# Positive part and square of the feed-forward rows in the halved chunks: from VectorE to ScalarE

## The chip, the cores and the metric

The kernel runs on one core of a Trainium2 chip. The metric is the device time of one execution in microseconds (us): the median of three runs of the kernel before is 2147.76 us (2145.67 to 2149.06). The engines are called as in the profile: PE is TensorE (matmuls; PEld are its weight loads), DVE is VectorE, ACT is ScalarE, POOL is GpSimd, SP is the engine that issues most of the loads.

## The reference

Two blocks of two layers each follow one another on 512 rows of width 1024, in float32: retention, latent attention, a chunk-gating mixer, dilated attention, each with its norms. In the second block each of the two layers ends with a feed-forward part, and this is what the change is about:

```python
y = _rms_norm(h, mlp_norm_g[layer])
h = h + jnp.square(jax.nn.relu(y @ w_up[layer])) @ w_down[layer]
```

The hidden width is 4096, so that the hidden rows are a 4096 x 512 matrix (features by positions), each element of which is cut at zero and squared between the two products.

## The kernel before, in words

Float32 accuracy is made of split operands: ACT rounds each operand to a high part (`hi`, a Copy to fp32r, line 1197), DVE (`lo`, line 1894) or, for weights, POOL (line 386) makes the low part as the difference, and PE adds three products (high with high, high with low, low with high). Weights come as 128x2048 panels: SP loads a panel into `RAW`, ACT writes `WH`, POOL writes `WL` in four parts of 128x512. There are two slots, used by turns.

The feed-forward part of a layer has 8 chunks of 512 hidden features. The first two are plain. The other six, the halved chunks, are made by a scheme with 7 products in place of 8 for each 256 features (`u` is 0 or 1). A halved chunk uses four panels: two up panels (u = 0, 1), then two down panels. Six halved chunks in each of two layers make 12. Of a chunk:

- PE runs `halved_panel` for u = 0 and u = 1, each with 7 products, then `down_panels`. The first down panel is taken by `tiles_together`: hidden tile k = 0 to 3 one after the other, 12 matmuls for each k, and before each k a wait until the low part of tile k (`HIDL`) is there. The second down panel follows without such waits.
- DVE runs `halved_up(i, 0)` and `halved_up(i, 1)`: it reads the products from the banks, adds them up into `T` (tile 0 and 1 for u = 0, tile 2 and 3 for u = 1; `near` is the first of the two and `far` the second), and cuts and squares each tile in place with one `scalar_tensor_tensor`, (max(t, 0)) * t, lines 2526 and 2532. Its signal `mlp_relu` counts these tiles. Between these steps it adds down results of the chunk before to `X` (line 2540), whose banks the u = 1 products want back, and in u = 1 it makes the low parts of tiles 0 and 1 (`low_hidden`), then those of tiles 2 and 3 at the end. After that it makes the sums of weight blocks for the next chunk (`sums_of_w`, lines 2478 to 2485).
- ACT takes its work in a written order: `WH` of the second up panel; `HIDH` of tile 0; `WH` of the first down panel; `HIDH` of tiles 1 and 2; `WH` of the second down panel; `HIDH` of tile 3; then the high parts of the weight sums (`EH`) with the next up panel between them.
- POOL makes `WL` of a panel in four parts as soon as ACT has its `WH`.

Behind the last halved chunk of the first of the two layers (L = 0) ACT also issues 16 DMAs of a bias table (`bias_table`, line 1693), then one more panel, and then the rows of the next norm (line 1265).

Of the kernel before, what the change touches and what calls it, by code (L numbers as in the profile page):

```python
# [146 lines left out]
def program(nc, panels, gains, xin, pin, pos, gn, decay, xtok, consts, every4, rel, onehot, wsT, bs, out, scratch, xsave):  # L147
    f32, f32r = mybir.dt.float32, mybir.dt.float32r
    ALU, ACT, AX = mybir.AluOpType, mybir.ActivationFunctionType, mybir.AxisListType
# [3 lines left out]
    with ctx:  # L153
        def sb(name, shape, dt=f32, c=ctx):
            return c.enter_context(nc.sbuf_tensor(name, shape, dt))

        S = Signals(lambda name: ctx.enter_context(nc.semaphore(name)))
# [34 lines left out]
        T = sb("T", [128, 4, 512])  # L192
# [1002 lines left out]
        def _(act):  # L1195
            def hi(dst, src):
                return nc.scalar.activation(dst, src, ACT.Copy)  # L1197
# [25 lines left out]
            def split_at(m):  # L1223
                split_panel(m, m % 2, m // 2)

            def split_in(i, per, m0):

                split_panel(i * per + m0, m0 % 2, i * (per // 2) + m0 // 2)
# [53 lines left out]
            def gained_tokens(L, rows):  # L1282
                for k in rows:
                    nc.scalar.activation(NORMED[:, k, :], X[:, k, :], ACT.Copy, scale=gain(f"mlp{L}", k))
                act.drain().then_inc(S["up_parts_hi"], 1)
# [401 lines left out]
            def mlp(L, n0):  # L1687
                def bias_table(kind):
                    rows = scratch[kind].rearrange("h q y -> h (q y)")
                    for b in range(128 // REPEATS):  # L1690
                        first = 127 - REPEATS * b
                        tile = rows[:, first:first + REPEATS * 255].rearrange("h (q y) -> q h y", y=255)[:, :, 0:128]
                        act.dma_start(TAB[REPEATS * b:REPEATS * b + REPEATS, :, KIND_AT[kind], :], tile)\
                           .then_inc(S["tab_loaded"], 16)

                def plain_chunk(c):
                    for f in range(4):
                        if f in (0, 3):
                            split_at(c * 4 + n0 + 2 + f // 3)
                        act.wait_ge(S["mlp_relu"], c * 4 + (4 * CHUNKS * L + f + 1))  # L1700
                        nc.scalar.activation(T[:, f, :], TG[:, f % 2, :], ACT.Square).then_inc(S["mlp_hid_f32"], 1)
                        act.drain()
                        hi(HIDH[:, f, :], T[:, f, :]).then_inc(S["mlp_hid_hi"], 1)
                        if c == 0 and f == 1:
                            gained_tokens(L, range(4, KD))

                def high_tokens():
                    act.wait_ge(S["up_parts_f32"], PARTS_SPLIT * L + 2)
                    hi(TOKH[:, :, :, :], TOK[:, :, :, :]).then_inc(S["up_parts_hi"], 1)

                def high_normed():
                    act.wait_ge(panel_used, n0 + 4 * PLAIN - 2)
                    hi(HH[:, 0:4, 0:256], NORMED[:, 0:4, 0:256])
                    hi(HH[:, 4:8, :], NORMED[:, 4:8, :]).then_inc(S["up_parts_hi"], 1)

                def high_sums(i, u):
                    act.wait_ge(S["up_parts_f32"], i * 2 + (PARTS_SPLIT * L + 3 + u))
                    hi(EH[:, u, :, :], SUMS[:, :, :]).then_inc(S["up_parts_hi"], 1)

                def high_of_chunk(i):  # L1720

                    high_sums(i, 0)
                    split_in(i, 4, n0 + 4 * PLAIN)
                    high_sums(i, 1)

                def halved_chunk(i):

                    def high_hidden(f):
                        act.wait_ge(S["mlp_relu"], i * 4 + (4 * CHUNKS * L + 4 * PLAIN + f + 1))
                        hi(HIDH[:, f, :], T[:, f, :]).then_inc(S["mlp_hid_hi"], 1)  # L1730

                    split_in(i, 4, n0 + 4 * PLAIN + 1)
                    high_hidden(0)
                    split_in(i, 4, n0 + 4 * PLAIN + 2)
                    high_hidden(1)
                    high_hidden(2)
                    split_in(i, 4, n0 + 4 * PLAIN + 3)
                    high_hidden(3)

                for c in range(PLAIN):  # L1740
                    plain_chunk(c)
                    if c == 0:
                        for j in range(2):
                            split_at(n0 + 4 + j)
                        high_tokens()
                high_normed()
                act.drain()
                high_of_chunk(0)
                with act.Fori(0, HALVES - 1) as i:
                    halved_chunk(i)  # L1750
                    high_of_chunk(i + 1)
                halved_chunk(HALVES - 1)
                if L == 0:
                    act.wait_ge(S["rows_stored"], 64)
                    for kind in range(4):
                        bias_table(kind)
                    split_at(n0 + 4 * CHUNKS)
# [132 lines left out]
        def _(ve):  # L1890
            v = nc.vector
# [527 lines left out]
            def mlp(L, n0):  # L2419
# [68 lines left out]
                def low_sums(i, u):  # L2488
                    ve.wait_ge(S["up_parts_hi"], i * 2 + (PARTS_HI * L + 5 + u))
                    lo(EL[:, u, :, :], SUMS[:, :, :], EH[:, u, :, :]).then_inc(S["up_parts_split"], 1)  # L2490

                def halved_up(i, u):
                    b0 = 4 - 4 * u
                    made, ahead = S["up_product"], 12 * HALVES * L + 6 * u
                    first, second, third = TG[:, u, 0:256], TG[:, u, 256:512], R[:, 256 * u:256 * u + 256]
                    near, far = T[:, 2 * u, :], T[:, 2 * u + 1, :]

                    def added(dst, b, to):

                        v.tensor_tensor(dst, B[b][:, 0:256], to, ALU.add)  # L2500
                        ve.drain()  # L2501
                        return v.tensor_tensor(dst, B[b][:, 256:512], dst, ALU.add)

                    ve.wait_ge(made, i * 12 + (ahead + 1))
                    v.reduce_sum(first, B[b0][:, :].rearrange("p (a n) -> p n a", a=2), AX.X)
                    ve.drain().then_inc(S["up_read"], 1)
                    if u == 0:
                        low_sums(i, 1)
                    ve.wait_ge(made, i * 12 + (ahead + 2))
                    added(second, b0 + 1, first).then_inc(free[b0 + 1], 1)  # L2510
                    ve.drain()
                    ve.wait_ge(made, i * 12 + (ahead + 3))
                    added(third, b0 + 3, second).then_inc(free[b0 + 3], 1)
                    ve.drain()
                    ve.wait_ge(made, i * 12 + (ahead + 4))
                    added(near[:, 256:512], b0 + 2, third).then_inc(S["up_read"], 1)
                    if u == 0:
                        down(i + (PLAIN - 1), 4, tiles=2)
                    else:
                        low_hidden(i * 4 + 4 * PLAIN, 0)  # L2520
                    ve.wait_ge(made, i * 12 + (ahead + 5))
                    v.reduce_sum(far[:, 0:256], B[b0][:, :].rearrange("p (a n) -> p n a", a=2), AX.X).then_inc(free[b0], 1)
                    ve.wait_ge(made, i * 12 + (ahead + 6))
                    added(near[:, 0:256], b0 + 1, third).then_inc(free[b0 + 1], 1)
                    ve.drain()
                    v.scalar_tensor_tensor(near, near, 0.0, near, ALU.max, ALU.mult).then_inc(S["mlp_relu"], 1)  # L2526
                    if u == 0:
                        down(i + (PLAIN - 1), 6, tiles=2)
                    ve.wait_ge(panel_used, i * 4 + (n0 + 4 * PLAIN + u + 1))
                    added(far[:, 256:512], b0 + 2, second).then_inc(free[b0 + 2], 1)  # L2530
                    ve.drain()
                    v.scalar_tensor_tensor(far, far, 0.0, far, ALU.max, ALU.mult).then_inc(S["mlp_relu"], 1)
                    if u == 1:
                        low_hidden(i * 4 + 4 * PLAIN, 1)

# [28 lines left out]
                with ve.Fori(0, HALVES - 1) as i:  # L2564
                    halved_up(i, 0)
                    halved_up(i, 1)
                    sums_of_w(i + 1, 0)
                    low_sums(i + 1, 0)
                    down(i + PLAIN, 0)
                    sums_of_w(i + 1, 1)  # L2570
# [413 lines left out]
```

## Time and profile before

| | |
|---|---|
| median of three runs | 2147.76 us (2145.67 to 2149.06) |
| the profiled execution's own time | 2148.23 us |
| its span | 2146.2 us |
| PE busy | 2116.5 us, 99% of the span |
| DVE busy | 1511.3 us, 70% |
| ACT busy | 914.6 us, 43% |
| POOL busy | 996.1 us, 46% |
| granted TensorE clock | full speed (2.4 GHz) over the whole span, 1.00 in the chunks looked at |

The chunks in question are at 1250 to 1491 us (first of the two layers) and 1891 to 2134 us (second). A row of the timeline gives start and duration in us, engine, line, operation, what it writes and reads, and, in brackets, how long the engine was idle before it and what ended that. Matmuls overlap, so a stalled PE shows little idle time in the busy columns: the distance of the same matmul from chunk to chunk is the better measure.

### The profile page before, as it was taken

Reading aid. Unit: us, or ns where it says so; the run is one execution under the profiler, and the core shown is the slowest. Engines: PE = TensorE matmul, PEld = TensorE weight load, DVE = VectorE, ACT = ScalarE, POOL = GpSimd, SP = SyncE. Lnnn points to the kernel's source line nnn. Section 1 sums busy time; section 2 is a strip of 40 time slices with the busy share of each in tenths; the row PEclk is TensorE's granted clock in tenths of the full one; section 3 lists DMA queues with packets and bytes.
Section 4 is the critical chain, followed back from the end, with each engine's and each line's share of the span. In section 5 each row is a group of like instructions: output and inputs, shape, how many; then the busy total and the mean of one; then the engine's idle time right before and its main releaser. Section 6 shows DMA issues by size and latency. Waiting matters only on the chain.

```text
span 2146.2 us, 30802 instructions
## 1 busy us (share of the span) xinstructions
PE 2116.5 (99%) x10510; PEld 1771.6 (83%) x10510; DVE 1511.3 (70%) x2143; ACT 914.6 (43%) x1315; POOL 996.1 (46%) x707
## 2 busy tenths in 40 slices
PE   9999999999999999999999999999999999999998
PEld 7888888778888888877888888888788888788886
DVE  7656556786777777778265788887565566788886
ACT  4433233555655555455445422224345445322233
POOL 4443544355434443425535655554443325555553
PEclk9999999999999999999999999999999999999999
DMA  6232222232222222232222222224212211222222
GB/s 227 87 103 83 95 74 91 89 126 101 87 78 78 78 78 81 87 117 97 100 79 98 98 98 98 98 98 137 98 66 73 79 60 59 98 98 99 97 99 77
DMA packets 38422, 202.16 MB, mean 94 GB/s; under 512 B 4395, under 2 KB 9643, under 8 KB 16076
## 3 DMA queue, kind: packets, MB, share of 16 engines
q1 hardware_dynamic: 29504, 191.46, 25.5%
q10 hardware_dynamic: 8844, 9.70, 1.5%
q8 instruction: 48, 0.79, 0.1%
q14 instruction: 26, 0.21, 0.0%
HBM read 195.90 MB, written 5.24 MB: 94 GB/s over the span
## 4 chain that ended last, share of the span: by engine, by line
PE 70%; DVE 15%; DVEq 7%; ACT 4%; issue 3%; POOL 1%; ACTq 1%; DMA 0%; POOLq 0%; SPq 0%
PE bank L468 12%; PE bank L474 11%; PE bank L469 11%; PE bank L455 8%; PE bank L456 8%; PE bank L457 8%; PE bank L947 2%; DVEq L2501 2%; DVEq L2482 1%; DVE X L2540 1%; PE bank L953 1%; DVE SUMS L2483 1%; ACT WH L1197 1%; ACT EH L1197 1%; DVE SUMS L1918 1%
## 5 line engine op out<-in xcount | busy, mean ns | idle before, releaser
L386 POOL TENSOR_TENSOR WL<-RAW,WH 128x512 fp32r<-128x512 f32 x700 | 989.8, 1446 | 1124.3 <-ACT WH L1197 1124.3
L1197 ACT ACTIVATE WH<-RAW 128x2048 fp32r<-128x2048 f32 (+1 forms) x190 | 336.4, 1773 | 239.1 <-PE bank L474 120.7
L468 PE MATMUL bank<-HB,WH 128*128 128x512 f32 x776 | 308.3, 397 | 0.8 <-DVEq L2595 0.8
L469 PE MATMUL bank<-HB,WH 128*128 128x512 f32 x776 | 302.8, 390 | 0.0
L474 PE MATMUL bank<-HB,WL 128*128 128x512 f32 x776 | 195.7, 395 | 0.0
L474 PEld LDWEIGHTS bank<-HB,WL 128*128 128x128 f32 x776 | 146.7, 189 | 32.7 <-issue 2.4
L468 PEld LDWEIGHTS bank<-HB,WH 128*128 128x128 f32 x776 | 146.0, 188 | 32.6 <-DVEq L2595 1.0
L469 PEld LDWEIGHTS bank<-HB,WH 128*128 128x128 f32 x776 | 145.9, 188 | 30.3 <-issue 1.0
L1197 ACT ACTIVATE HIDH<-T 128x512 fp32r<-128x512 f32 x64 | 40.2, 629 | 174.5 <-DVE T L2526 168.7
L1197 ACT ACTIVATE EH<-SUMS 128x1536 fp32r<-128x1536 f32 x24 | 35.7, 1489 | 175.3 <-DVEq L2486 175.3
L455 PE MATMUL bank<-HIDH,WH 128*128 128x512 f32 x256 | 100.5, 393 | 0.0
L457 PE MATMUL bank<-HIDH,WL 128*128 128x512 f32 x256 | 99.8, 390 | 0.0
L456 PE MATMUL bank<-HIDL,WH 128*128 128x512 f32 x256 | 99.7, 389 | 0.0
L468 PE MATMUL bank<-HIDH,WH 128*128 128x512 f32 x256 | 99.6, 389 | 0.0
L469 PE MATMUL bank<-HIDL,WH 128*128 128x512 f32 x256 | 99.6, 389 | 0.0
L2540 DVE TENSOR_TENSOR X<-X,bank 128x512 f32<-128x512 f32 x128 | 81.5, 680 | 8.6 <-PE bank L457 4.0
L1894 DVE TENSOR_TENSOR HIDL<-T,HIDH 128x512 fp32r<-128x512 f32 x64 | 68.2, 1081 | 24.9 <-ACT HIDH L1197 24.4
L947 PE MATMUL bank<-TOKB,EH 128*128 128x512 f32 x288 | 79.5, 397 | 0.9 <-DVE X L2540 0.5
L947 PE MATMUL bank<-HB,WH 128*128 128x512 f32 x288 | 78.4, 394 | 0.0
L455 PE MATMUL bank<-WH,HB 128*128 128x512 f32 x192 | 74.9, 390 | 0.7 <-ACT R L1197 0.7
L456 PE MATMUL bank<-WL,HB 128*128 128x512 f32 x192 | 74.7, 389 | 0.0
L457 PE MATMUL bank<-WH,HB 128*128 128x512 f32 x192 | 74.7, 389 | 0.0
(482 smaller groups left out, 5073.7 us busy)
## 6 DMA issues: line engine op xcount, KB each, us to landing
RAW<-panels SPq DMA_DIRECT2D x174, 1024.0 KB, 4.8
X<-xin SPq DMA_DIRECT2D x4, 512.0 KB, 8.0
xsave<-X ACTq DMA_DIRECT2D x4, 512.0 KB, 2.8
X<-xsave ACTq DMA_DIRECT2D x1, 2048.0 KB, 11.7
TAB<-scratch ACTq DMA_DIRECT2D x16, 128.0 KB, 3.3
out<-ACC SPq DMA_DIRECT2D x8, 256.0 KB, 2.3
RAW<-panels SPq DMA_DIRECT2D x2, 512.0 KB, 6.7
T<-xtok SPq DMA_DIRECT2D x2, 512.0 KB, 12.9
```

The lines of the kernel that those rows point to most:

```text
L386: gp.tensor_tensor(WL[:, s, cs], RAW[:, s, cs], WH[:, s, cs].bitcast(f32), ALU.subtract).then_inc(lo_ready, 1)
L455: nc.tensor.matmul(o, ah, bh, start=start, stop=False)
L456: nc.tensor.matmul(o, ah, bl, start=False, stop=False)
L457: return nc.tensor.matmul(o, al, bh, start=False, stop=stop)
L468: nc.tensor.matmul(o, wh[:, columns[k - k0]], xh[:, k, :], start=first and k == k0, stop=False)
L469: nc.tensor.matmul(o, wh[:, columns[k - k0]], xl[:, k, :], start=False, stop=False)
L474: end = nc.tensor.matmul(o, wl[:, columns[k - k0]], xh[:, k, :], start=False, stop=last and k == k1 - 1)
L947: nc.tensor.matmul(o[:, :].rearrange("p (a n) -> p a n", a=2), ah[:, cs], both(k), start=k == 0 and not onto, stop=k == 3, skip_group_chec ...
L1197: return nc.scalar.activation(dst, src, ACT.Copy)
L1894: return v.tensor_tensor(dst, src, high.bitcast(f32), ALU.subtract)
L2501: ve.drain()
L2540: end = v.tensor_tensor(X[:, f, :], X[:, f, :], B[b][:, :], ALU.add)
```

## The change

In `halved_up`, DVE no longer cuts and squares: a drain alone gives the signal `mlp_relu`, so this now says that the sums of the tile are in `T`. In `halved_chunk`, ACT does the work in two instructions in place, a Relu and a Square, each followed by a drain, ahead of the copy to `HIDH` that it made already. 48 `scalar_tensor_tensor` leave DVE (4 for each of 12 chunks), 96 activations come to ACT. The plain chunks, which already make the square on ACT, stay as they are.

```diff
                     def high_hidden(f):
                         act.wait_ge(S["mlp_relu"], i * 4 + (4 * CHUNKS * L + 4 * PLAIN + f + 1))
+                        nc.scalar.activation(T[:, f, :], T[:, f, :], ACT.Relu)
+                        act.drain()
+                        nc.scalar.activation(T[:, f, :], T[:, f, :], ACT.Square)
+                        act.drain()
                         hi(HIDH[:, f, :], T[:, f, :]).then_inc(S["mlp_hid_hi"], 1)
...
                     added(near[:, 0:256], b0 + 1, third).then_inc(free[b0 + 1], 1)
-                    ve.drain()
-                    v.scalar_tensor_tensor(near, near, 0.0, near, ALU.max, ALU.mult).then_inc(S["mlp_relu"], 1)
+                    ve.drain().then_inc(S["mlp_relu"], 1)
                     if u == 0:
                         down(i + (PLAIN - 1), 6, tiles=2)
                     ve.wait_ge(panel_used, i * 4 + (n0 + 4 * PLAIN + u + 1))
                     added(far[:, 256:512], b0 + 2, second).then_inc(free[b0 + 2], 1)
-                    ve.drain()
-                    v.scalar_tensor_tensor(far, far, 0.0, far, ALU.max, ALU.mult).then_inc(S["mlp_relu"], 1)
+                    ve.drain().then_inc(S["mlp_relu"], 1)
                     if u == 1:
                         low_hidden(i * 4 + 4 * PLAIN, 1)
```

On ACT, in the loop over halved chunks, from the second up panel to the copies of tiles 1 and 2, this is how the rows differ (+ is the changed kernel):

```order
 L1197 ACTIVATE WH<-RAW 128x2048
 L1729 REGISTER_ALU
+L1730 ACTIVATE T<-T 128x512
+L1732 ACTIVATE T<-T 128x512
 L1197 ACTIVATE HIDH<-T 128x512
 L1203 REGISTER_ALU
 L1197 ACTIVATE WH<-RAW 128x2048
 L1729 REGISTER_ALU
+L1730 ACTIVATE T<-T 128x512
+L1732 ACTIVATE T<-T 128x512
 L1197 ACTIVATE HIDH<-T 128x512
 L1729 REGISTER_ALU
```

The two new instructions stand ahead of each copy, and so ahead of the panel that follows it.

On DVE, at the end of u = 1, the rows before were these, from the sums of tile 2 to the first sum of weight blocks:

```order
L2502 TENSOR_TENSOR T<-bank,T 128x256
L2526 SCALAR_TENSOR_TENSOR T<-T 128x512
L2529 REGISTER_ALU
L2500 TENSOR_TENSOR T<-bank,TG 128x256
L2502 TENSOR_TENSOR T<-bank,T 128x256
L2532 SCALAR_TENSOR_TENSOR T<-T 128x512
L2439 REGISTER_ALU
L1894 TENSOR_TENSOR HIDL<-T,HIDH 128x512
L2439 REGISTER_ALU
L1894 TENSOR_TENSOR HIDL<-T,HIDH 128x512
L2477 ISA
L2478 TENSOR_TENSOR SUMS<-RAW 128x512
```

In the changed kernel (its lines stand 4 lower) the same place reads:

```order
L2506 TENSOR_TENSOR T<-bank,T 128x256
L2532 REGISTER_ALU
L2504 TENSOR_TENSOR T<-bank,TG 128x256
L2506 TENSOR_TENSOR T<-bank,T 128x256
L2443 REGISTER_ALU
L1898 TENSOR_TENSOR HIDL<-T,HIDH 128x512
L2443 REGISTER_ALU
L1898 TENSOR_TENSOR HIDL<-T,HIDH 128x512
L2481 ISA
L2482 TENSOR_TENSOR SUMS<-RAW 128x512
```

Nothing else has moved on DVE; the two low parts at the end now stand right behind the sums, and wait there for ACT.

## Rows read from the trace of the kernel before

**Rows 1.** The page's first part: busy us (share of span) xinstructions.

```profile
PE 2116.5 (99%) x10510; PEld 1771.6 (83%) x10510; DVE 1511.3 (70%) x2143; ACT 914.6 (43%) x1315; POOL 996.1 (46%) x707
```

**Rows 2.** Windows, first hidden matmul to the next chunk's: us, then PE, PEld, DVE, ACT, POOL.

```profile
1259.57:1301.07 41.50, 41.50 (x211) 35.17 (x209) 35.60 (x50) 12.62 (x10) 22.49 (x16) 1.00 0.29 101
1301.07:1343.05 41.98, 41.82 (x209) 35.33 (x209) 36.09 (x51) 12.61 (x10) 22.50 (x16) 1.00 0.29 100
...
1426.98:1468.76 41.78, 41.78 (x210) 35.34 (x209) 36.25 (x51) 12.61 (x10) 22.99 (x16) 1.00 0.29 100
sum 209.19, PE 208.74 PEld 176.51 DVE 180.08 ACT 63.08 POOL 112.91; mean PE 41.75 PEld 35.30 DVE 36.02 ACT 12.62 POOL 22.58
```

**Rows 3.** Timeline of PE, three places: start us, us, what, idle before.

```profile
1301.07 0.49 PE L455 MATMUL bank<-HIDH,WH 128*128 128x512 f32 x1
...
1309.35 0.39 PE L455 MATMUL bank<-HIDH,WH 128*128 128x512 f32 x1
...
1335.89 0.50 PE L947 MATMUL bank<-TOKB,EH 128*128 128x512 f32 x1 [0.16 <-DVE X L2540]
```

**Rows 4.** Timeline of DVE in the second halved chunk.

```profile
1291.96 0.69 DVE L2526 SCALAR_TENSOR_TENSOR T<-T 128x512 f32<-128x512 f32 x1
...
1299.28 2.26 DVE L1894 TENSOR_TENSOR HIDL<-T,HIDH 128x512 fp32r<-128x512 f32 x2
...
1302.55 0.42 DVE L2502 TENSOR_TENSOR T<-bank,T 128x256 f32<-128x256 f32 x1
...
1305.29 0.68 DVE L1894 TENSOR_TENSOR HIDL<-T,HIDH 128x512 fp32r<-128x512 f32 x1
1306.78 1.44 DVE L1894 TENSOR_TENSOR HIDL<-T,HIDH 128x512 fp32r<-128x512 f32 x1 [0.80 <-ACT HIDH L1197]
1308.39 1.52 DVE L2478 TENSOR_TENSOR SUMS<-RAW 128x512 f32<-128x512 f32 x1 [0.17 <-issue]
1309.84 1.77 DVE L2479 TENSOR_TENSOR SUMS<-RAW 128x512 f32<-128x512 f32 x1
...
1313.39 0.69 DVE L2485 TENSOR_TENSOR RAW<-RAW,SUMS 128x512 f32<-128x512 f32 x1
```

**Rows 5.** Timeline of ACT in the same chunk.

```profile
1293.23 1.90 ACT L1197 ACTIVATE WH<-RAW 128x2048 fp32r<-128x2048 f32 x1
...
1303.79 0.63 ACT L1197 ACTIVATE HIDH<-T 128x512 fp32r<-128x512 f32 x1 [7.66 <-DVE T L2526]
1304.33 1.90 ACT L1197 ACTIVATE WH<-RAW 128x2048 fp32r<-128x2048 f32 x1
1306.14 0.61 ACT L1197 ACTIVATE HIDH<-T 128x512 fp32r<-128x512 f32 x1
```

**Rows 6.** Timeline of POOL in the same chunk: the low parts of two panels.

```profile
1295.29 5.11 POOL L386 TENSOR_TENSOR WL<-RAW,WH 128x512 fp32r<-128x512 f32 x4 [3.83 <-ACT WH L1197]
...
1306.39 1.28 POOL L386 TENSOR_TENSOR WL<-RAW,WH 128x512 fp32r<-128x512 f32 x1 [6.00 <-ACT WH L1197]
```

**Rows 7.** Timeline of ACT in a plain chunk: Square, drain, copy.

```profile
1173.62 0.63 ACT L1701 ACTIVATE T<-TG 128x512 f32<-128x512 f32 x1
1174.34 0.63 ACT L1197 ACTIVATE HIDH<-T 128x512 fp32r<-128x512 f32 x1
```

**Rows 8.** Timeline of ACT behind the last halved chunk of L = 0.

```profile
1471.96 1.90 ACT L1197 ACTIVATE WH<-RAW 128x2048 fp32r<-128x2048 f32 x1
1473.05 0.85 ACTq L1693 DMA_DIRECT2D TAB<-scratch  x2
...
1481.04 1.92 ACT L1197 ACTIVATE WH<-RAW 128x2048 fp32r<-128x2048 f32 x1 [6.66 <-issue]
1482.86 0.70 ACT L1265 ACTIVATE HB<-X,G 128x512 fp32r<-128x512 f32 x1
```

**Rows 9.** Timelines of DVE and PE where that layer's next norm begins and ends.

```profile
1483.60 1.37 DVE L1907 SCALAR_TENSOR_TENSOR HB<-X,G,HB 128x512 fp32r<-128x512 f32 x1 [4.24 <-ACT HB L1265]
...
1503.33 1.13 PE L520 MATMUL bank<-SUMS,ONES 128*128 128x512 f32 x2 [0.62 <-DVEq L1920]
```

## The prediction

> **What bounds the kernel now.** The page's first part comes first: PE is busy for 99% of the span, DVE for 70%, ACT for 43% [rows 1]. That speaks for PE as the bound and for DVE and ACT work as free, and for most of the kernel it is so. It has to be checked in the halved chunks themselves, and busy shares don't do it, since overlapping matmuls hide a stall. So the second view is a table of windows, cut at the first matmul of each chunk that reads the hidden tiles [rows 2]. The first window lasts 41.50 us, the next three 41.98 (one row stands for them), the last 41.78. The work of PE is the same in all. So PE by itself needs about 41.4, and in steady state something else, slower by 0.5 us a chunk, sets the pace.
>
> The third view, PE's timeline, shows where: a product of u = 1 waits for a bank that DVE's L2540 gives back, and the first hidden matmul lasts 0.49 us in place of 0.39, as it is issued just when the low part of tile 0 has come [rows 3]. Fourth, the timelines of DVE, ACT and POOL in one chunk [rows 4 to 6]: DVE hardly waits for PE there; it goes round a ring of its own, with ACT and POOL in it: sums of a tile, square, ACT's copy, low part, weight sums, next chunk. This ring of 41.97 us is the bound, with PE half a microsecond behind. So the change is priced along the ring.
>
> **Price of a stage.** On ACT, Square, drain and copy follow each other by 0.72 us [rows 7]. A Relu has no row; I take it as another 128x512 activation with a drain, the same 0.72. Its bounds are 0.54 (the step from copy to the next panel without a drain, 1304.33 less 1303.79 [rows 5]) and 0.80 (the 0.70 of an activation with a scale for each partition [rows 8], and the 0.09 from end to start in rows 7). So the copy of a tile starts 1.44 us after the Relu does. On DVE a square takes 0.69 [rows 4]; I take back 0.15 to 0.2 for the signal, which now comes from a drain with a register step behind it (such gaps are 0.17 before L2478), so each removal frees about 0.5 us.
>
> **One chunk, step by step.** Let t = 0 be 1291.96, when DVE begins to square tile 0. The Relu begins there too, as the same drain releases it.
>
> First, before u = 1. ACT's copy of tile 0 starts at 1.44, and the panel behind it at 1.98 (it was 1293.23, so 1.27). POOL began 2.06 after that panel (1295.29) and takes four parts of 1.28, a little less back to back [rows 6]; now they end at about 5.3, 6.55, 7.8 and 9.05 if nothing comes between.
>
> Second, the low parts of tiles 0 and 1. DVE asked for the first at 1299.28, t = 7.32, in POOL's last part, and the two took 2.26. Two squares less bring this to about 6.26. That lies in POOL's second part. What happens then is read at the end of the chunk: the low part of tile 3, issued at 1306.78 during a POOL part that ended at 1307.67, lasted 1.44 instead of 0.68 and ended 0.55 after that part [rows 4, 6]. The next two DVE steps, 1.52 and 1.77, show the same again and again: the engines take turns, a DVE step ends 0.55 after the POOL part, and a POOL part 1.15 after the DVE step. So: low part 0 at 6.55 + 0.55 = 7.1, a POOL part to 8.25, low part 1 at 8.8. It was 1299.28 + 2.26, t = 9.58, so tile 2 is reached 0.77 earlier.
>
> The Trainium skill, page "SBUF — State Buffer", section "Who interferes with whom", says that a VectorE instruction with two SBUF inputs and a GpSimd instruction that reads SBUF exclude each other for a whole instruction, and that issue order decides who blocks. The trace agrees (1.44 against 0.68). By that rule POOL's third part, which waits first, goes in front of low part 1; the turn taken above rests on the rows.
>
> Third, tile 2. Its sums ended at 1302.97, t = 11.01; now 10.24. The Relu starts at 10.33, the copy at 11.77 (it was 11.83): two squares and a turn of POOL pay for the longer path. The second down panel starts at 12.31 (12.37).
>
> Fourth, tile 3: nothing pays here. Relu, Square and copy all stand behind that panel on ACT. The copy started 1.81 after the panel; now a Relu starts there, at 14.12, and the copy 1.41 later, ending at 16.16. Low part 3 then asks at 16.2, in POOL's second part (15.65 to 16.9), and ends at 17.46. Before, it ended at 1308.22, t = 16.26. So 1.2 us later.
>
> Fifth, the weight sums. They met three more POOL parts after low part 3, now two. Last sum: 17.46, POOL to 18.6, first sum 19.15, POOL 20.3, second 20.85, third 21.63, fourth 22.39. It was 22.12. The ring goes from 41.97 to 42.24, **0.27 us longer**, although DVE has 2.8 us less to do.
>
> **Sum.** Five passages between six chunks give 5 x 0.27 = 1.35 per layer. In the last chunk low part 3 is a further 1.2 later. Before, it ended 1.13 ahead of the matmul that waits for it (1309.35 [rows 3]), of which I leave 0.23 for signal and weight load, so 0.9 of cover. A layer's feed-forward part ends 1.35 + 1.2 - 0.9 = 1.65 later.
>
> For L = 0 another path is longer. ACT's 16 bias-table DMAs stood in front of a panel at 1481.04, and this in front of the next norm's rows, on which DVE waited 4.24 us and at whose end PE waits [rows 8, 9]. The first DMA went out 1.09 after the second down panel's start (1473.05), as soon as the copy of tile 3 was released. Now it also stands behind two drains: it goes out with that copy, 1.81 + 1.41 = 3.22 after the panel, 2.13 later. With 1.35 for the ring and 0.06 back, 3.4 us, which replaces 1.65.
>
> Together 3.4 + 1.65 = 5.05. The profiled execution took 2148.23 us (span 2146.2, the rest around it unchanged), 0.5 above the median; from the median 2147.76 this gives **2152.8 us**. Where bounds matter: a stage of 0.54 takes 0.5 off the copy of tile 3 and lets it meet the end of POOL's first part, so that the ring loses nothing (about +1); one of 0.80 puts 0.16 on tile 2 and on tile 3's copy, and the ring is some 0.2 to 0.3 longer still, +3 on the sum.
>
> **Rivals.**
> Fewer turns: low part 1 follows low part 0 without a POOL part between. Then it ends at 7.7, tile 2 is 1.1 us earlier still, the ring falls to 41.1 and PE's 41.4 becomes the bound. It gains 209.19 - 5 x 41.42 = 2.1 in each layer; the DMAs go out 1 us earlier than now. About 2144.7, faster than before. For it speaks that the two low parts followed each other at once in rows 4, against it that POOL had nothing left to do there, and that it had its turn between L2478 and L2479.
> A missed turn: if low part 0 asks 0.3 us later than reckoned, it misses the end of POOL's second part at 6.55 and waits for the third. Everything behind it comes 1.26 later, the ring is 43.5; 6 x 1.26 per layer, 15 more, 2168. The margin is 0.29 with a drain's gap uncertain by about 0.1 twice.
> Exchange at face value: each swap costs its own difference, 1.44 - 0.69, on tiles 2 and 3 of 12 chunks, 18 us, 2166. The Trainium skill, "ScalarE: Activation LUTs", section "Rules for kernel authors", gives relu, max and mul to VectorE and would point this way. Against it: the time that tile 2 gets back in the first to third steps.
> A cover that holds: ACT's stages are a bit shorter or DVE's relief a bit larger, so that ring and PE keep pace; only part of the DMAs' delay is left, 0 to +3, 2149.
>
> **How the numbers follow.** A measurement of this kernel tells 0.2%, 4.3 us, from no change. The forecast, +3 to +8, has a chance of 0.60, and 0.4 of this lies above 4.3 us. Fewer turns 0.14, of which 0.09 gains more than 4.3 us (the relief of L2540's banks adds to it); a missed turn 0.08; face value 0.04; a cover that holds 0.14. So slower 0.40 + 0.08 + 0.04, about 0.53; faster 0.09; within the bound 0.38. The range of the forecast alone is 2150.5 to 2156; 8 in 10 needs the cases beside it, 2145 to 2159.
>
> **What would show it.** The windows between first hidden matmuls are 42.2 us in steady state. The low part of tile 2 ends earlier against the first hidden matmul and that of tile 3 about 1 us later; PE now stalls before the first matmul of k = 3, and no more for L2540's bank. On DVE the low parts of tiles 0 and 1 have a POOL part between them. The first bias-table DMA goes out 3.2 us after the last panel's start instead of 1.09. Windows of 41.4 would show the ring gone and the forecast wrong; windows of 43.5 a missed turn; windows of 42.2 with an unchanged total would mean that the later path behind L = 0 has cover that I didn't see.

## The result and the profile after

The changed kernel takes 2153.95 us (median of seven runs, 2151.85 to 2155.46) against 2147.76 of the kernel before (seven runs, 2145.34 to 2149.06): a ratio of 1.003 with a 95% interval of 1.0021 to 1.0039, so between 4.5 and 8.4 us slower. The profiled execution took 2153.95 us with a span of 2151.9, 5.7 more than the span before. All lines of VectorE in this kernel stand 4 lower than before.

The page's first part, to be put beside [rows 1]:

```profile
PE 2116.9 (98%) x10510; PEld 1769.4 (82%) x10510; DVE 1474.6 (69%) x2095; ACT 974.1 (45%) x1411; POOL 1001.5 (47%) x707
```

DVE has 37 us less to do, ACT 60 more, PE the same. By busy time alone nothing is lost; in device time 6 us are. The windows from first hidden matmul to first hidden matmul, first of the two layers, answer to [rows 2]:

```profile
1258.94:1300.37 41.43, 41.43 (x211) 35.19 (x209) 32.02 (x46) 17.57 (x18) 22.12 (x17) 1.00 0.30 101
1300.37:1342.45 42.08, 41.71 (x210) 35.10 (x209) 32.68 (x47) 17.56 (x18) 22.80 (x17) 1.00 0.28 100
...
1384.63:1426.85 42.22, 41.73 (x211) 35.10 (x209) 32.81 (x47) 17.57 (x18) 22.92 (x17) 1.00 0.28 99
...
sum 210.08, PE 208.31 PEld 175.61 DVE 163.57 ACT 87.83 POOL 113.77; mean PE 41.66 PEld 35.12 DVE 32.71 ACT 17.57 POOL 22.75
```

The reader is to see that the windows have become longer (42.2 in place of 41.97) while of the engines' busy times in them only ACT's is clearly longer. PE, three places, beside [rows 3]:

```profile
1300.37 0.40 PE L455 MATMUL bank<-HIDH,WH 128*128 128x512 f32 x1
...
1309.11 0.49 PE L455 MATMUL bank<-HIDH,WH 128*128 128x512 f32 x1 [0.37 <-DVE HIDL L1898]
...
1335.44 1.09 PE L947 MATMUL bank<-TOKB,EH 128*128 128x512 f32 x4
```

The first hidden matmul no longer waits (0.40 in place of 0.49), nor does L947 for the bank of the down results; the matmul of k = 3 now does, for the low part of tile 3. It stands 8.74 us behind the first (1309.11 less 1300.37), where it would stand 8.21 behind without a stall (as in the experiment with tiles 0 and 1 below): 0.5 us in this chunk, 0.6 in the later ones. With the 0.1 that the stalled matmul itself lasts longer, this is nearly all that the windows have over PE's own 41.43. On DVE, ACT and POOL the second halved chunk reads as follows; the views are those of [rows 4 to 6].

```profile
1297.95 2.43 DVE L1898 TENSOR_TENSOR HIDL<-T,HIDH 128x512 fp32r<-128x512 f32 x2
...
1303.96 0.69 DVE L1898 TENSOR_TENSOR HIDL<-T,HIDH 128x512 fp32r<-128x512 f32 x1 [1.01 <-ACT HIDH L1197]
1307.68 1.30 DVE L1898 TENSOR_TENSOR HIDL<-T,HIDH 128x512 fp32r<-128x512 f32 x1 [3.03 <-ACT HIDH L1197]
...
1313.20 0.69 DVE L2489 TENSOR_TENSOR RAW<-RAW,SUMS 128x512 f32<-128x512 f32 x1
```

```profile
1291.59 0.63 ACT L1730 ACTIVATE T<-T 128x512 f32<-128x512 f32 x1 [5.72 <-DVEq L2529]
1292.29 0.63 ACT L1732 ACTIVATE T<-T 128x512 f32<-128x512 f32 x1
1292.99 0.63 ACT L1197 ACTIVATE HIDH<-T 128x512 fp32r<-128x512 f32 x1
1293.53 1.90 ACT L1197 ACTIVATE WH<-RAW 128x2048 fp32r<-128x2048 f32 x1
...
1301.89 0.63 ACT L1730 ACTIVATE T<-T 128x512 f32<-128x512 f32 x1 [4.54 <-DVEq L2529]
...
1303.83 1.90 ACT L1197 ACTIVATE WH<-RAW 128x2048 fp32r<-128x2048 f32 x1
1305.64 0.61 ACT L1730 ACTIVATE T<-T 128x512 f32<-128x512 f32 x1
...
1307.02 0.63 ACT L1197 ACTIVATE HIDH<-T 128x512 fp32r<-128x512 f32 x1
```

```profile
1295.59 5.95 POOL L386 TENSOR_TENSOR WL<-RAW,WH 128x512 fp32r<-128x512 f32 x4 [4.52 <-ACT WH L1197]
1305.89 5.93 POOL L386 TENSOR_TENSOR WL<-RAW,WH 128x512 fp32r<-128x512 f32 x4 [4.35 <-ACT WH L1197]
```

Two things are to be read here. POOL's four parts take 5.95 where they took 5.11, since DVE's two low parts now fall among them. And DVE, which waited 0.80 us for ACT before low part 3, waits 3.03: over the whole kernel these are the groups' rows of the low parts, before and after,

```profile
L1894 DVE TENSOR_TENSOR HIDL<-T,HIDH 128x512 fp32r<-128x512 f32 x64 | 68.2, 1081 | 24.9 <-ACT HIDH L1197 24.4
```

```profile
L1898 DVE TENSOR_TENSOR HIDL<-T,HIDH 128x512 fp32r<-128x512 f32 x64 | 69.3, 1096 | 63.9 <-ACT HIDH L1197 63.5
```

so DVE's busy time went down by 37 us, and as much has come back as a wait for ACT: 63.5 us in place of 24.4. ACT behind the last halved chunk of L = 0, beside [rows 8], and PE at the end of the next norm, beside [rows 9]:

```profile
1472.42 1.90 ACT L1197 ACTIVATE WH<-RAW 128x2048 fp32r<-128x2048 f32 x1
...
1475.63 8.33 ACTq L1693 DMA_DIRECT2D TAB<-scratch  x16
1484.06 1.92 ACT L1197 ACTIVATE WH<-RAW 128x2048 fp32r<-128x2048 f32 x1 [7.82 <-issue]
1485.88 0.70 ACT L1265 ACTIVATE HB<-X,G 128x512 fp32r<-128x512 f32 x1
```

```profile
1506.31 1.12 PE L520 MATMUL bank<-SUMS,ONES 128*128 128x512 f32 x2 [0.61 <-DVEq L1924]
```

The first DMA goes out 3.21 us behind the panel; panel, norm rows and the norm's end all come 3.0 later than before.

### The profile page after: what moved, and what is told of

Same layout as the page of the kernel before. It is cut to its first block, busy times and chain, and to the rows that moved or that the text cites. A ratio compares the mean times of both kernels' runs of the same rounds, so it can differ in the third digit from the quotient of the medians.

```text
span 2151.9 us, 30946 instructions
## 1 busy us (share of the span) xinstructions
PE 2116.9 (98%) x10510; PEld 1769.4 (82%) x10510; DVE 1474.6 (69%) x2095; ACT 974.1 (45%) x1411; POOL 1001.5 (47%) x707
## 4 chain that ended last, share of the span: by engine, by line
PE 69%; DVE 15%; DVEq 6%; ACT 4%; issue 3%; ACTq 2%; DMA 0%; POOL 0%; SPq 0%; POOLq 0%
PE bank L468 12%; PE bank L474 12%; PE bank L469 11%; PE bank L455 8%; PE bank L456 8%; PE bank L457 8%; PE bank L947 2%; DVEq L2505 2%; DVE HIDL L1898 1%; DVEq L2486 1%; ACT EH L1197 1%; PE bank L953 1%; DVE SUMS L1922 1%; ACTq L1731 1%; DVE X L2542 1%
## 5 line engine op out<-in xcount | busy, mean ns | idle before, releaser
L1898 DVE TENSOR_TENSOR HIDL<-T,HIDH 128x512 fp32r<-128x512 f32 x64 | 69.3, 1096 | 63.9 <-ACT HIDH L1197 63.5
L1730 ACT ACTIVATE T<-T 128x512 f32<-128x512 f32 x48 | 29.9, 623 | 123.3 <-DVEq L2529 123.3
L947 PE MATMUL bank<-TOKB,EH 128*128 128x512 f32 x288 | 78.6, 394 | 0.0
L947 PE MATMUL bank<-HB,WH 128*128 128x512 f32 x288 | 78.4, 394 | 0.0
```

The source lines that it names most:

```text
L947: nc.tensor.matmul(o[:, :].rearrange("p (a n) -> p a n", a=2), ah[:, cs], both(k), start=k == 0 and not onto, stop=k == 3, skip_group_chec ...
L1898: return v.tensor_tensor(dst, src, high.bitcast(f32), ALU.subtract)
```

## The experiments

Six kernels were run, each timed in five rounds against the kernel before (2147.88 us median in the first four, 2147.85 in the last two). The changed kernel was not timed again beside them: where a run is compared with its 2153.95 us, this rests on the kernel before, whose three medians agree to 0.12 us.

**Tile 3 alone.** The theory was that the loss comes from tile 3, whose three steps on ACT stand behind the second down panel; the rival was that it comes from the longer path of all four.

```diff
+ON_ACT = (3,)
...
-                        nc.scalar.activation(T[:, f, :], T[:, f, :], ACT.Relu)
+                        if f in ON_ACT:
+                            nc.scalar.activation(T[:, f, :], T[:, f, :], ACT.Relu)
...
-                    ve.drain().then_inc(S["mlp_relu"], 1)
+                    if 2 * u + 1 in ON_ACT:
+                        ve.drain().then_inc(S["mlp_relu"], 1)
+                    else:
+                        ve.drain()
+                        v.scalar_tensor_tensor(far, far, 0.0, far, ALU.max, ALU.mult).then_inc(S["mlp_relu"], 1)
```

> Only tile 3 of each halved chunk is cut and squared by ScalarE; tiles 0 to 2 stay on VectorE. Ring theory: tile 3 is the only tile whose longer path nothing pays for, so this fourth of the change shows all of the loss: low part 3 ends 1.26 us later, in POOL's second part, the ring goes from 41.97 to 42.3 us, the first bias-table DMA of L = 0 goes out 3.2 us after the last panel's start. 5 x 0.33 + 1.26 - 0.9 = 2.0 for L = 1, 1.65 + 2.13 = 3.8 for L = 0: about 2153.5. Rival (each swapped tile costs its share of the 6.2 us): a fourth, 2149.3.

Measured: 2155.1 us (2153.16 to 2155.93), ratio 1.0032 (1.0020 to 1.0044). One tile of four makes the whole loss. The time is 1.6 above the 2153.5 expected and far from the 2149.3 of equal shares; that it lies 1.2 above that of the whole change is within the two intervals. Windows, then PE's matmul of k = 3 in the chunk of 1344.02:

```profile
1344.02:1386.33 42.31, 42.10 (x209) 35.23 (x209) 34.41 (x50) 13.89 (x12) 22.05 (x16) 1.00 0.28 99
```

```profile
1352.56 0.49 PE L456 MATMUL bank<-HIDH,WH 128*128 128x512 f32 x1
```

It stands 8.54 behind the first hidden matmul. The other stalls of [rows 3] are still there as well, since nothing has relieved DVE ahead of tile 2.

**All but tile 3.** The same code, with

```diff
-ON_ACT = (3,)
+ON_ACT = (0, 1, 2)
```

> Tiles 0, 1 and 2 on ScalarE as in the changed kernel, tile 3 back on VectorE. Ring theory: tile 2's path is paid by the two squares less ahead of it and by one turn of POOL, low part 3 meets POOL's first part again and ends where it did before, the ring is 41.9 us and the DMAs go out as before: about 2147, no loss. Rival of equal shares: three fourths of the loss, 2152.4.

Measured: 2145.11 us (2144.12 to 2146.78), ratio 0.9989 (0.9980 to 0.9998): 2.7 us faster than before, 8.8 faster than the whole change, and 1.9 below the 2147 expected. The windows, of the first and of the fourth passage,

```profile
1258.95:1300.38 41.43, 41.43 (x211) 35.18 (x210) 34.12 (x47) 16.31 (x16) 22.90 (x17) 1.00 0.29 101
...
1383.65:1425.51 41.86, 41.66 (x210) 35.24 (x209) 34.55 (x48) 16.32 (x16) 23.33 (x17) 1.00 0.28 100
```

show that PE alone sets the pace at first and the ring then falls behind by 0.4 a chunk: better than the 41.97 of before, not free.

**Tiles 0 and 1 alone.** Here ACT has no square between two panels, and DVE loses the two squares that stand ahead of tile 2.

```diff
-ON_ACT = (3,)
+ON_ACT = (0, 1)
```

> Only tiles 0 and 1 (u = 0) on ScalarE, tiles 2 and 3 on VectorE. Ring theory: tile 2 is reached 0.77 us earlier than before and its path is not longer, so the ring falls to about 41.2 us, below PE's 41.42, and PE becomes the bound: windows of 41.4 between first hidden matmuls, 2.1 us less for each layer and some tenths more behind L = 0, about 2143.2, faster than both kernels. Rival of equal shares: half of the loss, 2150.9.

Measured: 2141.92 us (2141.22 to 2142.01), ratio 0.9970 (0.9960 to 0.9981). This version beats both kernels, by 6.0 us the one before and by 12.0 the changed one. In all ten windows of both layers the pace is PE's own:

```profile
1300.66:1342.09 41.43, 41.43 (x211) 35.19 (x209) 35.01 (x49) 15.03 (x14) 23.42 (x17) 1.00 0.28 101
...
sum 207.13, PE 207.13 PEld 175.91 DVE 175.20 ACT 75.19 POOL 117.06; mean PE 41.43 PEld 35.18 DVE 35.04 ACT 15.04 POOL 23.41
```

DVE at the end of the chunk before 1342.09 and behind it (lines here stand 2 lower than in the changed kernel):

```profile
1338.92 2.38 DVE L1900 TENSOR_TENSOR HIDL<-T,HIDH 128x512 fp32r<-128x512 f32 x2
...
1345.06 0.68 DVE L1900 TENSOR_TENSOR HIDL<-T,HIDH 128x512 fp32r<-128x512 f32 x1
1346.54 1.45 DVE L1900 TENSOR_TENSOR HIDL<-T,HIDH 128x512 fp32r<-128x512 f32 x1 [0.80 <-ACT HIDH L1198]
```

Low part 3 ends 5.90 us behind the first hidden matmul (1346.54 + 1.45 less 1342.09), and is wanted at 8.21. In the changed kernel it ends at 8.6 (1307.68 + 1.30 less 1300.37). From the three versions, what each move is worth: tiles 0 and 1 give 6.0 us, tile 2 takes back 3.2 (2145.11 less 2141.92), tile 3 another 8.8.

**Low parts 0 and 1 in one instruction.** The whole change, with one turn of POOL taken away.

```diff
-                        low_hidden(i * 4 + 4 * PLAIN, 0)
+                        ve.wait_ge(S["mlp_hid_hi"], i * 4 + 4 * PLAIN + (at + 2))
+                        lo(HIDL[:, 0:2, :], T[:, 0:2, :], HIDH[:, 0:2, :]).then_inc(S["mlp_hid_split"], 2)
```

> The whole change, but the low parts of tiles 0 and 1 are one instruction of 128x1024, so that POOL can't take a turn between them. If the turn matters as the forecast has it: the pair ends at t = 7.65 in place of 8.8, tile 2 is reached 1.15 us earlier still, the ring falls to 41.1 us and PE's 41.42 is the bound; the later DMAs stay. About 2144.5. If the turns are nothing and tile 3's place behind the panel is the whole of it: as the changed kernel, 2154.

Measured: 2145.27 us (2143.21 to 2147.04), ratio 0.9988 (0.9979 to 0.9997). The two low parts take 1.26 us in place of 2.43, and the ring no longer sets the pace. First the low parts, then POOL's third part of the panel beside them, then the windows:

```profile
1339.76 1.26 DVE L1898 TENSOR_TENSOR HIDL<-T,HIDH 128x1024 fp32r<-128x1024 f32 x1
```

```profile
1339.90 2.28 POOL L386 TENSOR_TENSOR WL<-RAW,WH 128x512 fp32r<-128x512 f32 x1
```

```profile
sum 207.16, PE 207.16 PEld 175.95 DVE 159.23 ACT 87.90 POOL 115.29; mean PE 41.43 PEld 35.19 DVE 31.85 ACT 17.58 POOL 23.06
```

POOL's part now waits for the whole of the joint low part, 2.28 us in place of 1.28 [rows 6], and DVE hardly waits. With all four tiles on ACT, then, one turn between POOL and DVE is enough to decide whether the ring or PE sets the pace. It also shows that the first rival of the prediction (fewer turns) was priced to 0.6 us, 2144.7, and that its condition was what failed.

**The bias-table DMAs earlier.** In the last halved chunk of L = 0 tile 3 goes back to DVE.

```diff
-                halved_chunk(HALVES - 1)
+                halved_chunk(HALVES - 1, (0, 1, 2) if L == 0 else (0, 1, 2, 3))
...
+                    if not last_of_first:
+                        ve.drain().then_inc(S["mlp_relu"], 1)
+                    else:
+                        ve.drain()
+                        v.scalar_tensor_tensor(far, far, 0.0, far, ALU.max, ALU.mult).then_inc(S["mlp_relu"], 1)
```

> The whole change, but in the last halved chunk of L = 0 tile 3 is cut and squared by VectorE as before, so that ScalarE reaches the 16 bias-table DMAs without a Relu and a Square in front of them. Theory (the DMAs stand on the path of the next norm): the first DMA goes out about 1.1 us after the last panel's start instead of 3.2, and all that follows comes 2.1 us earlier: 2153.95 - 2.1 = 2151.8; chunk windows stay at 42.2. Rival (that path has cover, and L = 0 lost its 3.6 us through the chunks and the last low part): the low part of tile 3 in one chunk comes 1.2 us earlier, of which 0.5 us was seen as a stall: 2153.4.

Measured: 2149.5 us (2148.24 to 2150.63), ratio 1.0005 (0.9996 to 1.0014), 4.4 faster than the whole change, where 2.1 had been expected; the windows stayed at 42.2. ACT there, and DVE's square of tile 3:

```profile
1472.04 0.35 ACTq L1693 DMA_DIRECT2D TAB<-scratch  x1
1472.18 1.90 ACT L1197 ACTIVATE WH<-RAW 128x2048 fp32r<-128x2048 f32 x1
...
1474.30 6.07 ACTq L1693 DMA_DIRECT2D TAB<-scratch  x12
1480.47 1.92 ACT L1197 ACTIVATE WH<-RAW 128x2048 fp32r<-128x2048 f32 x1 [5.87 <-PE bank L457]
1482.29 0.70 ACT L1265 ACTIVATE HB<-X,G 128x512 fp32r<-128x512 f32 x1
```

```profile
1471.31 0.69 DVE L2539 SCALAR_TENSOR_TENSOR T<-T 128x512 f32<-128x512 f32 x1
```

The theory held and its size did not. The first DMA goes out when DVE's square of tile 3 has ended, at 1472.00, and that is 0.14 us ahead of the panel, not 1.1 behind it: tile 2, and the panel behind it, are late on ACT, tile 3 is not late on DVE. Against the panel this is 3.35 earlier than the 3.21 of the changed kernel. The last panel still starts 0.10 behind the last DMA issue (1474.30 + 6.07), as it does there (1475.63 + 8.33), though the row names PE as the releaser; the norm rows come at 1482.29, 3.6 earlier. So the rival (cover) is out, and this path is worth 3.6 of the 4.4; the other 0.8 was not traced.

**Tile 3 ahead of the panel.** The whole change with two lines of ACT's order exchanged.

```diff
-                    split_in(i, 4, n0 + 4 * PLAIN + 3)
                     high_hidden(3)
+                    split_in(i, 4, n0 + 4 * PLAIN + 3)
```

> The whole change with one order turned round on ScalarE: Relu, Square and copy of tile 3 ahead of the high part of the second down panel instead of behind it. Theory (what costs time is that tile 3's three steps stand behind that panel, so that its low part, asked for in POOL's second part, holds up the weight sums): the copy ends about 1.9 us earlier, low part 3 and the first weight sum run before POOL begins the panel, the ring falls below PE's own need, windows 41.4 us as with tiles 0 and 1 alone; the bias-table DMAs go out about 1 us later than in the kernel before; 2143.5. Rival (the panel, now 1.9 us later, is what PE waits for next): its low part comes 1 to 2 us late in every chunk, windows 42.4 or more, 2153 or above.

Measured: 2145.69 us (2142.27 to 2148.34), ratio 0.9987 (0.9978 to 0.9996): the order alone turns a loss of 6 us into a gain of 2. The time is 2.2 above the 2143.5 expected. Eight of the ten windows are 41.43, two (one in each layer) are 42.0, and DVE shows why; low parts 0 and 1 of the fourth and of the fifth halved chunk, POOL's four parts beside them, and the windows from these chunks:

```profile
1380.88 2.38 DVE L1898 TENSOR_TENSOR HIDL<-T,HIDH 128x512 fp32r<-128x512 f32 x2
...
1422.31 3.53 DVE L1898 TENSOR_TENSOR HIDL<-T,HIDH 128x512 fp32r<-128x512 f32 x2
```

```profile
1378.38 6.04 POOL L386 TENSOR_TENSOR WL<-RAW,WH 128x512 fp32r<-128x512 f32 x4 [4.80 <-ACT WH L1197]
...
1419.79 5.51 POOL L386 TENSOR_TENSOR WL<-RAW,WH 128x512 fp32r<-128x512 f32 x4 [4.80 <-ACT WH L1197]
```

```profile
1384.05:1425.48 41.43, 41.43 (x211) 35.19 (x209) 31.97 (x45) 17.56 (x18) 23.49 (x17) 1.00 0.29 101
1425.48:1467.52 42.04, 41.75 (x211) 35.16 (x209) 33.13 (x47) 17.56 (x18) 22.46 (x16) 1.00 0.28 100
```

DVE asks 3.17 us ahead of the first hidden matmul both times. POOL began 5.67 ahead of it in the one, 5.69 in the other, and on this side of 0.02 POOL's third part comes first when its second ends: the two low parts take 1.15 longer. In L = 1 two decimals don't tell the chunk that misses the turn from one that meets it: in both DVE asks 2.51 behind POOL's start (1978.40 less 1975.89, and 1936.97 less 1934.46). This is the missed turn of the prediction's second rival, at a price of 0.6 a chunk here, as the ring was that much shorter than PE's own time there.

## Why the prediction was right

The time forecast, 2152.8, stands 1.15 below the measured one, and the steps of the working can be laid beside the trace one by one. With t = 0 at 1291.59, the start of the first Relu:

| step | forecast | measured |
|---|---|---|
| copy of tile 0 / panel behind it | 1.44 / 1.98 | 1.40 / 1.94 |
| POOL's first part begins | 4.04 | 4.00 |
| DVE asks for low part 0 | 6.26 | 6.36 |
| both low parts made | 8.8 | 8.79 |
| Relu of tile 2 | 10.33 | 10.30 |
| second down panel | 12.31 | 12.24 |
| Relu of tile 3 / end of its copy | 14.12 / 16.16 | 14.05 / 16.06 |
| low part 3 made | 17.46 | 17.39 |
| last weight sum ends | 22.39 | 22.30 |
| ring | 42.24 | 42.17 to 42.22 |

Each measured value but the ring is a row's start, or start and duration, in the fences of this chunk above, less 1291.59; the ring is the last three windows (the second is 42.08).

**Price of a stage.** Forecast 0.72, measured 0.70, from Relu to Square and from Square to copy. The first step had the bounds 0.54 and 0.80.

**The turns.** The rule that an engine's step and POOL's parts take turns carried the whole working, and it held: low parts 0 and 1 lasted 2.43 us with a part of POOL between. The joint instruction, which takes this turn away and saves little else (1.26 us, where two low parts that wait for nothing take 0.69 each), moved the windows from 42.2 to 41.43. The Trainium skill, "SBUF — State Buffer", section "Who interferes with whom", tells of exclusion for a whole instruction; that agrees with POOL's part of 2.28 us behind the joint low part. That DVE asked in time for this turn was a closer thing than the prediction had it. It reckoned a margin of 0.29; POOL's second part is the row

```profile
1296.84 1.30 POOL L386 TENSOR_TENSOR WL<-RAW,WH 128x512 fp32r<-128x512 f32 x1
```

and ends at 1298.14, 0.19 behind DVE's asking at 1297.95. With tile 3 ahead of the panel, two chunks of twelve did miss the turn.

**Tile 2 and tile 3.** "Two squares and a turn of POOL pay" for tile 2, "nothing pays" for tile 3: this is shown. Tile 3 alone lost 7.2 us, all but tile 3 gained 2.7 (with tile 2 in it, which by itself takes back 3.2 of what tiles 0 and 1 give), and with tile 3 moved ahead of the panel the whole change gains 2.2. That the loss comes from where the work stands in ACT's order, and not from ACT being slower at it, is shown by this last one: same instructions, other order.

**The sum.** Its terms, in the profiled executions:

- Up to the first hidden matmul: forecast 0, measured -0.63 (1258.94 less 1259.57 of [rows 2]).
- L = 0, from there to the end of the next norm: forecast 3.4, measured 3.61 (1506.31 less 1503.33 of [rows 9], and 0.63). Inside it two misses nearly cancel, so that the fit is in part luck: the five windows grew by 0.89 (210.08 less 209.19), not by 1.35, and the stretch behind them by 2.72, not by 2.1. Part of this is where PE's mark stands: from ACT's second down panel of one chunk to that of the next the ring is 41.91 before (1304.33 to 1471.96, four passages) and 42.15 after (1303.83 to 1472.42), 0.24 longer where 0.27 was forecast. That the DMAs carry the stretch behind the windows is shown by the experiment that gave 3.6 back (more than was lost, as the DMAs there went out ahead of the panel).
- From there to the last matmuls, with L = 1 in it: forecast 1.65, measured 1.82 (2140.97 less 2136.17 in the rows below, 4.80, less 2.98).
- The last matmuls themselves: forecast 0, measured 0.93. The last PE rows of the kernel before and of the changed one, and the windows over them with the granted clock (third column from the end):

```profile
2136.17 2.82 PE L544 MATMUL bank<-CONST,RC 128*128 128x128 f32 x16 [0.69 <-issue]
```

```profile
2140.97 3.75 PE L544 MATMUL bank<-CONST,RC 128*128 128x128 f32 x16 [0.69 <-issue]
```

```profile
2136.20:2138.90 2.70, 2.70 (x16) 2.50 (x16) 1.56 (x3) 0.00 (x0) 0.00 (x0) 0.68 0.00 0
```

```profile
2141.00:2144.70 3.70, 3.70 (x16) 3.43 (x16) 1.64 (x3) 0.00 (x0) 0.00 (x0) 0.50 0.02 7
```

The clock granted to the last 16 matmuls is a mix of both levels before (0.68) and 1.2 GHz throughout after (0.50); in both, PE had been mostly idle in the 4 us ahead of them, with eight matmuls of two columns in between. The four terms make 5.73, the difference of the spans. What failed is small: the 0.93 at the end and the 0.63 at the start were not in the sum, and nothing in the change explains either. The one at the start arises before 37 us, where both kernels do the same work: from 7.44 to 10.60 us PE's matmuls of 128x512 last 0.63 in the kernel before, and 0.39 to 0.40 at the same place in the changed one. The four terms together are 0.7 above the 5.05 of the forecast. The other 0.5 of the 1.15 is the profiled execution of the kernel before, 0.5 above its kernel's median, while that of the changed kernel stands at its median.

That the loss itself is not one of the clock is seen by taking executions of the same mean granted clock. At 0.995 those of the kernel before, beside the experiments, have a mean of 2149.0 us (twelve) and those of the changed kernel 2154.7 (four); at 0.997 it is 2145.5 (nine) and 2152.6 (two).

**What the prediction did not see.** It looked for one sign for the whole change. It had the parts of opposite sign in hand (tile 2 paid for by relief on DVE, tile 3 not) and did not go on to what half of the change would give, 6 us. The Trainium skill, "ScalarE: Activation LUTs", section "Rules for kernel authors", gives relu and mul to VectorE; for the time of this kernel, the runs agree with it for tiles 2 and 3 and not for tiles 0 and 1, where VectorE is in the ring that sets the pace and ScalarE has time (2141.92 us with these two on ScalarE, 2147.88 with none).

**What stays open.** Tiles 0 and 1 alone gain 6.0, and the windows explain 4.2 of it (207.13 against 209.19 in [rows 2] for L = 0, and 207.13 against 209.25 in L = 1). The table of the kernel before has the clock at full speed over the whole span; this is not quite so, its mean over that execution is 0.996. In the attention part between the two layers the granted clock over one stretch of 60 us is 0.91 before and 0.94 in that version,

```profile
1790.00:1850.00 60.00, 55.62 (x231) 45.56 (x230) 40.60 (x33) 25.38 (x28) 34.21 (x20) 0.91 0.25 88
```

```profile
1790.00:1850.00 60.00, 55.32 (x239) 45.05 (x238) 39.86 (x34) 25.22 (x26) 35.52 (x22) 0.94 0.25 88
```

which is up to 0.03 x 60 = 1.8 us of full speed, and would be the rest. The executions of the kernel before point the same way: their mean is 2150.9 us at a mean granted clock of 0.994 (six) and 2145.6 at 0.997 (five), in the rounds beside this version, six of whose eight executions have 0.997 and a mean of 2141.9. At the same clock, then, it gains 3.7, near the 4.2 of the windows. But its two executions at 0.995 and 0.996 took no longer (2142.00 and 2141.22). Whether the clock comes with the version or by chance of the execution, no run here tells.

## What to carry to other kernels

Where engines go round in a ring, price a moved instruction by what stands next to it on both engines. Here work that left VectorE ahead of a step that others wait for was a gain, work that arrived behind a long instruction on ScalarE was a loss, and the tiles of one loop could be given to different engines. Look at what else stands in the receiving engine's queue, DMA issues above all: here 16 of them, at one place of the program, passed on 2.1 us, a third of the loss. And when a change has parts of both signs, run the good half.

## What had not been expected of the hardware

Who is first between POOL and DVE can hang on hundredths of a microsecond: with POOL's start 0.02 us earlier, 2.38 us became 3.53, and one and the same kernel falls to either side from chunk to chunk. And DMA issues on ACT's queue go ahead of activations that stand before them in its order and have not begun (1472.04 against 1472.18). They do wait for drains ahead of them: in the changed kernel, with two drains in front, the first goes out at 1475.63, behind Relu and Square of tile 3.
